# Four edits in a two-block fp32 transformer kernel: one attention stage for three branches, middle taps on ScalarE, key weights loaded once for two heads, modulation sums in the up part

## The chip, the cores and the metric

The kernel runs on one core of a Trainium2 chip, as one launch. The metric is the device time of the launch in microseconds (us). TensorE (PE) multiplies, VectorE (DVE) and ScalarE (ACT) compute elementwise, GpSimd (POOL) computes elementwise and issues some DMAs, SyncE (SP) issues the other DMAs. Each engine runs its own queue in order, and the engines meet at semaphores.

## The reference, cut to what matters

All tensors are fp32, with 256 context tokens, 256 latent tokens and a width of 1024. A first block has two decoder layers; each ends in a feed-forward net with a depthwise 3x3 convolution:

```python
def conv_ffn(h, w_up, conv_w, conv_b, w_down, grid):
    gate, up = jnp.split(h @ w_up, 2, axis=-1)
    gate = dwconv_grid(gate, conv_w, conv_b, grid)
    return (jax.nn.gelu(gate, approximate=True) * up) @ w_down
```

Layer 0 does it for 512 tokens, layer 1 for the 256 latent tokens. A second block has one layer of sparse attention with a SwiGLU net, and one layer whose attention has three branches over the same queries, 16 heads of 64 with 4 key heads:

```python
pc = masked_softmax(sc, cmp_end[None, :] <= t[:, None])   # 15 compressed keys
oc = jnp.einsum('bgrqn,bngd->bgrqd', pc.astype(vc.dtype), vc)
...
o = gb[..., 0:1] * oc.astype(F32) + gb[..., 1:2] * os_.astype(F32) + gb[..., 2:3] * ow.astype(F32)
```

At this length the selected branch and the window branch both see all earlier tokens. A mixture of experts follows. Every layer also needs its modulation vectors, `silu(c) @ w_ada[layer] + b_ada[layer]`, with a weight of 1024 x 6144.

## The kernel before, in words

The program is a chain of stages (`engines_block`). In a stage each engine has its own list of work; between stages all engines meet.

**Feed-forward, `ffn_stage` (L1677).** The up part runs 11 rounds. A round loads four weight tiles of 512 KB (two for the gate chunks in banks 0 and 1, two for the up chunks in banks 2 and 3) and PE fills banks 0 and 1, then 2 and 3. DVE copies the nine taps and the bias of a chunk out of `vec` (L1731, L1732), writes the middle tap and the bias (`tensor_scalar`, L1737), adds the eight other taps one after the other (L1747; with context tokens two more, L1739 and L1740), and frees the bank. ScalarE applies gelu (L1771), and DVE multiplies with bank 2 or 3 (L1756) and frees that. For layer 0 (`split`, 512 tokens) each weight tile is also cut into a high and a low part, by DVE (L246) and POOL (L298). PE may start on a bank only when it has been freed, and in the next round it wants bank 1 a quarter of a half-round after bank 0. The down part is `gemm_stage` (L953) with 4 rounds of four tiles.

**Modulation sums, `ModSums` (L526).** 12 groups of 512 columns; a group has 4 tiles of 512 KB that POOL loads into a ring (L559), and 8 `scalar_tensor_tensor` of 128x512 on DVE (L573), each waiting for the one before. For layer 1 of the first block all 12 groups run beside the down part (`in_background`). In `swiglu_stage` they run beside its up part. `mod_stage` (L714) then turns the sums.

**Small projections, `small_stage` (L2479).** For keys ("pair") the weight is laid out with the columns of a head twice, `[P, DC, n, 2, HD]`, so that one matmul group of 8 steps writes the head into both halves of the partitions; it takes 16 DMAs of 128 KB with runs of 64 numbers, ahead of which PE doesn't start, and one group for each head. Five key tensors of 4 heads and one of 1 head are made so: one of 4 and the one of 1 in the sparse layer, `k_cmp` and `v_cmp` in one stage, `k_slc` and `k_win` in the next.

**Attention, `attention_stage` (L2626).** 16 items, each a query block `b` and a pair of heads: `b`=0 has 128 keys, `b`=1 has 256, the compressed branch has 16 for both. PE scores (L2655), DVE scales, masks and takes the maximum (L2732, L2734), ScalarE takes the exponential (L2705), DVE divides and gates (L2719 to L2724), PE transposes (L2666), ScalarE copies (L2690), PE multiplies with the values (L2676), and ScalarE copies the output (L2697) or DVE adds it (L2740). DVE's order within step n is: norm of item n-1, mask of item n, output of item n-3. The branch layer calls the stage three times.

## Time and profile before

| | us |
|---|---|
| median of 3 runs | 4150.27 (4146.25 to 4158.99) |
| the profiled execution, its own time | 4148.6 |
| its span | 4146.7 |
| PE busy | 3445.2 (83%) |
| DVE busy | 2622.0 (63%) |
| ACT busy | 1443.2 (35%) |
| POOL busy | 1145.1 (28%) |
| mean granted TensorE clock | 0.898 of full |

A busy share is a mean over some hundred stages with different limits. What a stage is worth is read from that stage's own rows. Clock 1.00 is TensorE at 2.4 GHz, 0.50 is 1.2 GHz.

### The profile page before, as it was taken

How to read it: one execution, taken by the hardware profiler on the slowest of the kernel's cores; microseconds unless marked ns; L12 is line 12 of the kernel's file. 1: busy time of each engine (PE TensorE's matmuls, PEld its weight loads, DVE VectorE, ACT ScalarE, POOL GpSimd, SP SyncE). 2: the span in 40 equal slices, each digit the busy share in tenths (PEclk: the TensorE clock that was granted, in tenths of full speed). 3: DMA queues.
4: the chain of work that ended last, by engine and by line, in shares of the span. 5: the costliest groups of instructions: out<-in, count | busy, mean ns of one | idle time of the engine just before them, and what ended most of it. 6: DMA issues, size and time to landing. Idle time of an engine off the chain costs nothing. (4 is left out here: it accounts for less than half of the span.)

```text
span 4146.7 us, 71734 instructions
## 1 busy us (share of the span) xinstructions
PE 3445.2 (83%) x26140; PEld 2695.3 (65%) x26140; DVE 2622.0 (63%) x4214; ACT 1443.2 (35%) x2628; POOL 1145.1 (28%) x1074
## 2 busy tenths in 40 slices
PE   5897867999687888598576887777769999999997
PEld 2644446864464787487464776675547888888886
DVE  2437668889556445566545440235449999999997
ACT  1124321000205664100102100013237777777775
POOL 0000004432001220101200110000027778787785
PEclk8998978999799999799786998966879999999998
DMA  7310013247120000446531773320139999999995
GB/s 296 94 51 1 1 41 96 92 144 244 42 82 21 5 5 4 147 143 228 206 78 35 236 263 110 88 74 1 41 124 334 354 335 343 345 337 348 335 342 215
DMA packets 335179, 651.12 MB, mean 157 GB/s; under 512 B 68413, under 2 KB 193449, under 8 KB 334825
## 3 DMA queue, kind: packets, MB, share of 16 engines
q1 hardware_dynamic: 311193, 561.84, 39.6%
q0 software_dynamic: 23040, 83.90, 5.9%
q8 instruction: 160, 2.62, 0.3%
q10 hardware_dynamic: 720, 2.23, 0.1%
q14 instruction: 66, 0.54, 0.0%
HBM read 646.85 MB, written 1.05 MB: 156 GB/s over the span
## 5 line engine op out<-in xcount | busy, mean ns | idle before, releaser
L3279 DVE TENSOR_TENSOR weights_lo<-raw_ring,weights_hi 128x704 fp32r<-128x704 f32 (+1 forms) x376 | 451.4, 1242 | 58.5 <-ACT weights_hi L3240 57.7
L3161 POOL TENSOR_TENSOR weights_lo<-raw_ring,weights_hi 128x192 fp32r<-128x192 f32 (+1 forms) x376 | 403.8, 1088 | 120.9 <-ACT weights_hi L3240 95.5
L3240 ACT ACTIVATE weights_hi<-raw_ring 128x896 fp32r<-128x896 f32 (+1 forms) x376 | 364.1, 986 | 140.1 <-PE bank_pair L3216 129.9
L3216 PE MATMUL bank_pair<-weights_hi,expert_x_hi 128*128 128x512 f32 (+1 forms) x1024 | 308.6, 382 | 29.7 <-POOL weights_lo L3161 21.9
L323 PE MATMUL bank_pair<-H,ring_up 128*128 128x256 f32 x1408 | 310.8, 383 | 22.6 <-DMA ring_up<-in_ffn_w_gate 10.3
L323 PEld LDWEIGHTS bank_pair<-H,ring_up 128*128 128x128 f32 x1408 | 269.2, 192 | 63.8 <-DMA ring_up<-in_ffn_w_gate 10.5
L3279 DVE TENSOR_TENSOR weights_lo<-H,weights_hi 128x704 fp32r<-128x704 f32 (+1 forms) x240 | 292.5, 1261 | 16.4 <-ACT weights_hi L3240 16.4
L3216 PE MATMUL bank_pair<-weights_lo,expert_x_hi 128*128 128x512 f32 (+1 forms) x1024 | 294.5, 368 | 0.0
L3216 PE MATMUL bank_pair<-weights_hi,expert_x_lo 128*128 128x512 f32 (+1 forms) x1024 | 293.8, 368 | 0.0
L323 PE MATMUL bank_pair<-x_hi,ring_hi_in 128*128 128x512 f32 (+1 forms) x576 | 209.6, 364 | 94.6 <-DVE ring_lo_in L298 81.9
L3161 POOL TENSOR_TENSOR weights_lo<-H,weights_hi 128x192 fp32r<-128x192 f32 (+1 forms) x240 | 258.7, 1090 | 67.5 <-ACT weights_hi L3240 56.5
L3240 ACT ACTIVATE weights_hi<-H 128x896 fp32r<-128x896 f32 (+1 forms) x240 | 236.2, 993 | 71.7 <-PE bank_pair L3216 71.7
L323 PE MATMUL bank_pair<-ffn_h,ring_down 128*128 128x512 f32 (+1 forms) x704 | 235.6, 497 | 21.3 <-DMA ring_down<-in_ffn_w_down 17.1
L895 POOL TENSOR_TENSOR norm_work<-X 128x512 f32<-128x512 f32 x7 | 8.2, 1170 | 886.3 <-SPq L196 886.3
L3216 PEld LDWEIGHTS bank_pair<-weights_hi,expert_x_hi 128*128 128x128 f32 x1024 | 175.8, 189 | 79.8 <-DVE weights_lo L3279 28.5
L323 PEld LDWEIGHTS bank_pair<-ffn_h,ring_down 128*128 128x128 f32 x704 | 136.3, 195 | 120.2 <-issue 89.0
L323 PE MATMUL bank_pair<-x_lo,ring_hi_in 128*128 128x512 f32 (+1 forms) x576 | 205.6, 357 | 0.0
L323 PE MATMUL bank_pair<-x_hi,ring_lo_in 128*128 128x512 f32 (+1 forms) x576 | 205.5, 357 | 0.0
L3216 PEld LDWEIGHTS bank_pair<-weights_lo,expert_x_hi 128*128 128x128 f32 x1024 | 186.3, 188 | 24.5
L3216 PEld LDWEIGHTS bank_pair<-weights_hi,expert_x_lo 128*128 128x128 f32 x1024 | 186.7, 188 | 23.8
L323 PEld LDWEIGHTS bank_pair<-x_hi,ring_hi_in 128*128 128x128 f32 x576 | 113.6, 197 | 117.2 <-DVE ring_lo_in L298 85.0
L559 POOL DMA_DIRECT2D mod_ring_ada<-in_w_ada x96 | 69.4, 723 | 376.3 <-DVE mod_sums_ada L573 188.3
(632 smaller groups left out, 7409.0 us busy)
## 6 DMA issues: line engine op xcount, KB each, us to landing
raw_ring<-in_moe_w_gate SPq DMA_DIRECT2D x72, 896.0 KB, 6.7
raw_ring<-in_moe_w_up SPq DMA_DIRECT2D x64, 896.0 KB, 6.5
ring_up<-in_ffn_w_up SPq DMA_DIRECT2D x110, 512.0 KB, 3.5
mod_ring_ada<-in_w_ada POOLq DMA_DIRECT2D x96, 512.0 KB, 6.7
raw_ring<-in_moe_w_down SPq DMA_DIRECT2D x48, 1024.0 KB, 7.3
H<-in_moe_w_gate SPq DMA_DIRECT2D x40, 896.0 KB, 6.9
H<-in_moe_w_up SPq DMA_DIRECT2D x40, 896.0 KB, 6.1
H<-in_moe_w_down SPq DMA_DIRECT2D x32, 1024.0 KB, 7.6
```

The costliest lines, as they stand in the source:

```text
L323: ins = self.core.nc.tensor.matmul(self.banks[o][:, 0:moving.shape[1]], lhs, moving, start=(s == self.first[o] and k == 0 and i == 0), sto ...
L559: eng.dma_start(self.ring[:, s], self.w[:, k:k + self.PART, ds(g * self.WIDE, self.WIDE)]).then_inc(self.landed[s].sem, 16)
L895: nc.gpsimd.tensor_tensor(work[0][:, q], jobs[0].x(q), jobs[0].x(q), ALU.mult).then_inc(pool_squared.sem, 1)
L3161: nc.gpsimd.tensor_tensor(lo[:, u % CUTS, at].bitcast(F32R), raw_part(u)[:, at], hi[:, u % CUTS, at], ALU.subtract).then_inc(pool_parted.s ...
L3216: ins = nc.tensor.matmul(banks[half][:, 0:b - a], x, w[:, a:b], start=start and i == 0, stop=stop and i == 2)
L3240: nc.scalar.activation(hi[:, u % CUTS, 0:n].bitcast(F32R), raw_part(u), ACT.Copy).then_inc(cut.sem, 1)
L3279: nc.vector.tensor_tensor(lo[:, u % CUTS, 0:n].bitcast(F32R), raw_part(u)[:, 0:n], hi[:, u % CUTS, 0:n], ALU.subtract).then_inc(dve_parted ...
```

## The change

1. `ffn_stage`, both layers: the taps of both chunks are copied first; ScalarE writes the middle tap and the bias (Identity with a scale and a bias operand) and signals DVE, which adds the other taps. Gelu follows as before.
2. `ffn_stage`, layer 1 only: 11 of the 12 groups of modulation sums move from the down part to the up part, one group a round, in two halves of four, each ahead of one multiplication; POOL issues their loads there. One group stays beside the down part.
3. `small_stage`: key weights are loaded once, with one DMA of 1 MB; one matmul group makes two heads, and ScalarE copies each head into both halves, four copies a group.
4. `attention_stage`: the three branches are items of one stage (48 items), their outputs add up in PSUM; DVE masks item n before it norms item n-1; PE transposes item n-2 and multiplies item n-3; score tiles are threefold. The value matmuls have 64 columns a head, into one half of the output each. The sparse layer has 16 items and gets the same order.
5. In the branch for overfull experts a norm is added.

```diff
-                    c.ended(nc.vector.tensor_copy(taps[:, o, 9:10], st.vec[:, ds(b0 + n, 1)]))
-                    bank = g.wait_bank(dve, o, it)
-                    if not first:
-                        dve.wait_ge(gelu_ready.sem, gelu_ready.at(it * 2 + o - 1))
+                    nc.vector.tensor_copy(taps[:, o, 9:10], st.vec[:, ds(b0 + n, 1)]).then_inc(taps_ready.sem, 1)
+                for o in (0, 1):
+                    bank = g.banks[o]
+                    dve.wait_ge(middle_ready.sem, middle_ready.at(it * 2 + o + 1))
                     y = conv[:, o]
-                    c.ended(nc.vector.tensor_scalar(y, bank[:, 0:T], taps[:, o, 4:5], taps[:, o, 9:10], ALU.mult, ALU.add))
...
                 ahead(1)
                 for o in (0, 1):
+                    if sums:
+                        sums.add_group(dve, it, range(4 * o, 4 * o + 4))
                     bank = g.wait_bank(dve, 2 + o, it)
...
+                for o in (0, 1):
+                    act.wait_ge(taps_ready.sem, taps_ready.at(it * 2 + o + 1))
                     if not first:
                         act.wait_ge(g.free[2 + o].sem, g.free[2 + o].at(it))
+                    bank = g.wait_bank(act, o, it)
+                    nc.scalar.activation(conv[:, o], bank[:, 0:T], ACT.Identity, scale=taps[:, o, 4:5], bias=taps[:, o, 9:10]).then_inc(middle_ready.sem, 1)
+                for o in (0, 1):
+                    act.wait_ge(g.free[o].sem, g.free[o].at(it + 1))
                     nc.scalar.activation(gelu[:, o], conv[:, o], ACT.Gelu_apprx_tanh).then_inc(gelu_ready.sem, 1)
...
-    sums = beside()
+    if sums:
+        sums.part(n_it, sums.total)
+    else:
+        sums = beside()
...
+        def both_halves(bank, dst, g, heads):
+            for j in range(heads):
+                for half in (0, 1):
+                    ins = nc.scalar.activation(dst[half * HD:(half + 1) * HD, g + j], bank[j * HD:(j + 1) * HD], ACT.Copy)
...
-                t = core.sb(f"w_pair{i}", [P, DC, n, 2, HD], ctx=ctx)
+                t = core.sb(f"w_pair{i}", [P, DC, n * HD], ctx=ctx)
+                for g in range(0, n, 2):
...
-                if kind == "pair":
-                    for k in range(DC):
-                        for a in (0, 1):
-                            loaded[i].count(sp.dma_start(ws[i][:, k, :, a], ...), 16)
+                width = n if kind == "tokens" else n * HD
+                loaded[i].count(sp.dma_start(ws[i][:], v[:, :, col:col + width]), 16)
...
+            for n in range(N + 3):
                 if n < N:
+                    score(n)
+                if 0 <= n - 2 < N:
+                    turn(n - 2)
+                if 0 <= n - 3:
+                    add(n - 3)
...
+                        ins = nc.tensor.matmul(OUT[g % 2][h * HD:(h + 1) * HD, 0:P], br.v[0:w, j, hp * 2 // group, HD:2 * HD], pt[0:w, n % 2, h * 2 + j],
+                                               start=i == 0 and j == 0, stop=i == B - 1 and j == last)
...
+            for n in range(N + 4):
+                if 0 <= n - 2 < N:
+                    copy_turned(n - 2)
+                if n < N:
+                    expo(n)
+                if 0 <= n - 4 and (n - 4) % B == B - 1:
+                    copy_out((n - 4) // B)
...
+            for n in range(N + 1):
+                if n < N:
+                    mask(n)
+                if n:
+                    norm(n - 1)
...
+        attention_stage(core, st, q, [Branch(kc, vc, cmp_neg, CMP_STRIDE, branch(0), cmp_seen), Branch(k_slc, v_slc, seen, gate=branch(1)),
+                                      Branch(k_win, v_win, seen, gate=branch(2))], out)
```

## Rows read from the trace of the kernel before

**Rows 1.** Windows of both up parts: busy of each engine, clock, DMA.
```profile
core 0: us, PE busy (x) PEld busy (x) DVE busy (x) ACT busy (x) POOL busy (x), PEclk, DMA share, GB/s
660.00:890.00 230.00, 228.85 (x1010) 189.18 (x1008) 202.59 (x344) 13.85 (x22) 102.63 (x40) 1.00 0.27 85
...
1760.00:1920.00 160.00, 154.27 (x699) 132.14 (x698) 99.61 (x261) 8.86 (x22) 0.00 (x0) 1.00 0.43 134
```

**Rows 2.** Timeline, layer 1's up part: start, length, instruction, idle before.
```profile
1766.68 0.54 DVE L1737 TENSOR_SCALAR conv<-bank_pair,taps 128x256 f32<-128x256 f32 x1 [12.53 <-PE bank_pair L323]
1767.25 3.70 DVE L1747 SCALAR_TENSOR_TENSOR conv<-bank_pair,taps,conv 128x189 f32<-128x189 f32 x8
...
1775.46 14.08 PE L323 MATMUL bank_pair<-H,ring_up 128*128 128x256 f32 x64 [0.27 <-DVE conv L1747]
1789.92 10.41 PE L323 MATMUL bank_pair<-H,ring_up 128*128 128x256 f32 x47 [0.38 <-DVE conv L1747]
...
1920.41 0.42 DVE L1756 TENSOR_TENSOR ffn_h<-conv,bank_pair 128x256 f32<-128x256 f32 x1 [0.23 <-ACT conv L1771]
```

**Rows 3.** Eight sum steps in the timeline; Identity of 256 columns in the groups.
```profile
2002.93 6.27 DVE L573 SCALAR_TENSOR_TENSOR mod_sums_ada<-mod_ring_ada,act,mod_sums_ada 128x512 f32 x8 [1.32 <-DMA mod_ring_ada<-in_w_ada]
...
L836 ACT ACTIVATE H<-norm_work,mod,coef 128x256 f32<-128x256 f32 x72 | 36.1, 586 | 24.6 <-DVE norm_work L885 24.6
```

**Rows 4.** Timeline: PE's start in layer 1's up part and in SwiGLU's.
```profile
1757.46 17.73 PE L323 MATMUL bank_pair<-H,ring_up 128*128 128x256 f32 x72 [8.65 <-DMA ring_up<-in_ffn_w_up]
...
2314.03 31.23 PE L323 MATMUL bank_pair<-H,ring_up 128*128 128x256 f32 x135 [10.31 <-DMA ring_up<-in_ffn_w_gate]
```

**Rows 5.** Timeline: layer 1's down part, and the first matmuls behind it.
```profile
1925.36 15.79 PE L323 MATMUL bank_pair<-ffn_h,ring_down 128*128 128x256 f32 x64 [7.42 <-DMA ring_down<-in_ffn_w_down]
...
1971.74 19.26 PE L323 MATMUL bank_pair<-ffn_h,ring_down 128*128 128x256 f32 x88 [0.60 <-ACT Y L1777]
...
2032.61 3.64 PE L743 MATMUL bank_pair<-mod_sums_ada,const 128*32 128x512 f32 x16 [21.76 <-PEq L196]
```

**Rows 6.** Timeline, layer 0's up part: a copy of taps while POOL computes.
```profile
872.00 2.36 DVE L1731 COPY taps<-vec 128x9 f32<-128x9 f32 x1
```

**Rows 7.** Small projections: timeline of SP and PE, and a DMA's landing.
```profile
2111.71 8.61 SPq L2512 DMA_DIRECT2D w_pair<-in_a_w_in  x16
...
2123.11 15.79 PE L2531 MATMUL bank_pair<-H,w_pair 128*128 128x256 f32 x64 [12.91 <-DMA w_pair<-in_a_w_in]
...
2589.99 29.98 PE L2531 MATMUL bank_pair<-H,w_pair 128*128 128x256 f32 x128 [15.94 <-DMA w_pair<-in_w_kv]
...
w_tokens<-in_w_kv SPq DMA_DIRECT2D x1, 1024.0 KB, 6.5
```

**Rows 8.** Windows of attention, columns as in Rows 1.
```profile
2211.46:2225.03 13.57, 11.15 (x50) 8.77 (x50) 6.73 (x20) 6.38 (x29) 0.00 (x0) 0.50 0.00 0
2245.63:2255.85 10.22, 5.91 (x44) 4.68 (x44) 6.43 (x13) 5.21 (x18) 0.00 (x0) 1.00 0.00 0
2817.28:2848.98 31.70, 27.37 (x120) 18.28 (x120) 11.98 (x72) 13.32 (x72) 0.00 (x0) 0.50 0.00 1
2855.73:2861.29 5.56, 3.32 (x16) 2.47 (x16) 3.02 (x11) 2.29 (x10) 0.00 (x0) 0.50 0.00 0
...
2206.22:2259.90 53.68, 39.23 (x208) 29.55 (x208) 28.20 (x64) 26.13 (x97) 0.00 (x0) 0.69 0.00 1
2807.69:2963.95 156.26, 110.32 (x576) 80.72 (x576) 84.03 (x288) 64.85 (x257) 0.00 (x0) 0.68 0.00 1
2231.97:2235.84 3.87, 3.13 (x12) 2.19 (x13) 2.15 (x5) 1.74 (x6) 0.00 (x0) 0.50 0.00 0
```

**Rows 9.** The window in which the clock rises in the sparse layer's attention.
```profile
2238.00:2243.00 5.00, 3.79 (x24) 2.54 (x22) 2.98 (x6) 2.52 (x10) 0.00 (x0) 0.87 0.00 0
```

**Rows 10.** Timeline: PE's value and score matmuls of one step at clock 0.50.
```profile
2217.95 1.06 PE L2676 MATMUL bank_pair<-pt,v 128*128 128x128 f32 x4
2218.94 0.80 PE L2655 MATMUL bank_pair<-kd,q 64*128 64x128 f32 x4
```

More of the change, by code:

```diff
@@ L2524, in _ @@
         def _(pe):
-            for m, (i, operands, width, _) in enumerate(outs):
+            for m, (i, operands, rows, width, _) in enumerate(outs):
                 pe.wait_ge(loaded[i].sem, loaded[i].at(loaded[i].n))
@@ L2530, in _ @@
                     lhs, rhs = operands(k)
-                    ins = nc.tensor.matmul(core.bank(m % 4)[:, 0:width], lhs, rhs, start=k == 0, stop=k == DC - 1)
+                    ins = nc.tensor.matmul(core.bank(m % 4)[0:rows, 0:width], lhs, rhs, start=k == 0, stop=k == DC - 1)
                 ready.count(ins)
@@ new lines, in score @@
+            def score(n):
+                b, hp, i = items[n]
+                br = branches[i]
+                if n >= 2:
+                    pe.wait_ge(masked.sem, masked.at(n - 1))
+                for h in (0, 1):
+                    half = slice(h * HD, (h + 1) * HD)
+                    ins = nc.tensor.matmul(SC[n % 2][:, h, 0:br.keys(b)], q[half, hp, b * P:(b + 1) * P],
+                                           br.k[half, hp * 2 // group, 0:br.keys(b)], start=True, stop=True)
+                ins.then_inc(scored.sem, 1)
@@ new lines, in turn @@
+            def turn(n):
+                b, hp, i = items[n]
+                pe.wait_ge(normed.sem, normed.at(n + 1))
+                if n >= 2:
+                    pe.wait_ge(pt_ready.sem, pt_ready.at(n - 1))
+                for h in (0, 1):
+                    for j, (at, w) in enumerate(branches[i].blocks(b)):
+                        ins = nc.tensor.transpose(TR[n % 2][0:w, (h * 2 + j) * P:(h * 2 + j + 1) * P], s[:, n % 3, h, at:at + w], st.C("ident"))
+                ins.then_inc(turned.sem, 1)
@@ new lines, in add @@
+            def add(n):
+                b, hp, i = items[n]
+                br, g = branches[i], n // B
+                pe.wait_ge(pt_ready.sem, pt_ready.at(n + 1))
+                if i == 0 and g >= 2:
+                    pe.wait_ge(out_taken.sem, out_taken.at(g - 1))
+                last = len(br.blocks(b)) - 1
+                for j, (_, w) in enumerate(br.blocks(b)):
+                    for h in (0, 1):
+                        ins = nc.tensor.matmul(OUT[g % 2][h * HD:(h + 1) * HD, 0:P], br.v[0:w, j, hp * 2 // group, HD:2 * HD], pt[0:w, n % 2, h * 2 + j],
+                                               start=i == 0 and j == 0, stop=i == B - 1 and j == last)
+                ins.then_inc(summed.sem, 1)
@@ new lines, in copy_out, with expo @@
+            def copy_out(g):
+                b, hp = pairs[g]
+                act.wait_ge(summed.sem, summed.at((g + 1) * B))
+                nc.scalar.activation(out[:, hp, b * P:(b + 1) * P], OUT[g % 2][:, 0:P], ACT.Copy).then_inc(out_taken.sem, 1)
+            def expo(n):
+                b, hp, i = items[n]
+                act.wait_ge(masked.sem, masked.at(n + 1))
+                if n >= 2:
+                    act.wait_ge(normed.sem, normed.at(n - 1))
+                for h in (0, 1):
+                    x = s[:, n % 3, h, 0:branches[i].keys(b)]
+                    ins = nc.scalar.activation(x, x, ACT.Exp, bias=low[:, n % 2, h:h + 1], accum_out=total[:, n % 2, h:h + 1])
+                ins.then_inc(exped.sem, 1)
@@ new lines, in norm @@
+            def norm(n):
+                b, hp, i = items[n]
+                br = branches[i]
+                K = br.keys(b)
+                x, r = s[:, n % 3, :, 0:K], total[:, n % 2]
+                dve.wait_ge(exped.sem, exped.at(n + 1))
+                c.ended(nc.vector.reciprocal(r, r))
+                if br.gate is not None:
+                    c.ended(nc.vector.tensor_tensor(r, r, br.gate[:, b, 2 * hp:2 * hp + 2], ALU.mult))
+                if br.some is not None:
+                    c.ended(nc.vector.tensor_tensor(x, x, br.some[:, b, 0:K].unsqueeze(1).to_broadcast([P, 2, K]), ALU.mult))
+                nc.vector.tensor_tensor(x, x, r.unsqueeze(2).to_broadcast([P, 2, K]), ALU.mult).then_inc(normed.sem, 1)
```

192 lines of the change are left out of this document (74 added, 118 removed).

## The prediction, on record before the result was known

> **What bounds the kernel now.** I read the page first, then the windows of each stage that the diff touches, then the timeline inside it. The page's shares decide nothing here: every edited stage has its own limit.
>
> Layer 0's up part is PE's: 228.85 us busy of 230.00, clock full; DVE has 202.59 [rows 1]. Layer 1's up part is nearly PE's: a round starts every 14.46 us (1775.46 to 1789.92), of which 14.08 is matmul and 0.38 a wait for DVE's last tap [rows 2]. Between bank-ready and that last tap DVE does two middle taps of 0.54 and two chains of 3.70. DVE is busy 99.61 of 160 us there and the DMA engines 0.43 of the time [rows 1], so there is room for something. In layer 1's down part PE has done its four rounds 21.76 us before the next matmul, which comes at 2032.61 [rows 5]: PE idles there while the sums finish. The small projections wait 11.4 us for sixteen DMAs (2111.71 to 2123.11) [rows 7]. Attention is a serial round trip: in five items of 128 keys DVE is busy 6.73 of 13.57 us, ACT 6.38, PE 11.15 at half clock; in three items of 256 keys at full clock nobody is busy more than 6.43 of 10.22 [rows 8].
>
> **Attention.** The new order lets DVE mask item n while ScalarE is at item n-1, so the round trip goes and the busiest engine sets the pace. DVE's busy time an item, plus 0.1 for gaps between dependent instructions (an estimate): 128 keys 6.73/5+0.1=1.45; gated 3.02/2+0.1=1.61; 256 keys 6.43/3+0.1=2.24, gated some 2.4; compressed 11.98/12+0.1=1.1 [rows 8]. ScalarE has 6.38/5=1.28, 5.21/3=1.74 and 13.32/12=1.11, less than DVE over a triple. PE is the question: at half clock it has 11.15/5=2.23 an item of 128 keys and 27.37/12=2.28 a compressed one, more than DVE; at full clock 5.91/3=1.97 even for 256 keys, less [rows 8]. Its value matmuls now fill half the array's columns each: of the 2.23 the value step is 0.99 (2217.95 to 2218.94) [rows 10]. It costs between half of that, if the two halves run side by side as the two heads' scores do (four score records in 0.80 [rows 10]), and all of it; I take 1.9 an item. The clock stood at 0.50 through the whole compressed stretch, but rose some 30 us into the sparse stage (0.87 in 2238 to 2243 [rows 9]), with PE still pausing there. PE will now pause less; I take 20 us at half clock in the sparse stage and 25 in the branch stage.
>
> The Trainium skill, TensorEngine Tiling, Theoretical Speedup, says that a stationary side of at most 64 columns gives up to twice the speed. By it the value step would be 0.5 and the item 1.7, 2 to 3 us less over both stages; the rows here show no such matmul.
>
> Start and end of a stage: 53.68 less eight items of 2.71 and eight of 3.41 leaves 4.7 [rows 8], kept. Sparse: 8x1.45+8x2.24+4.7=34.2, and for the slow clock 8x0.45+1.3=4.9 more: 39.1, against 53.68, so -14.6. Branch: a triple is 1.1+2x1.61=4.3 or 1.1+2x2.4=5.9; 8x(4.3+5.9)+4.7=86.3, and four triples at half clock (2.28+2x1.9=6.1) cost 1.8 each: 93.5, against 156.26, so -62.8. Together -77.4. Ends: full clock from the start -89; half clock throughout (2.23 and, from the 3.87 window with its 3.13 of PE, 3.6 an item [rows 8]) only -24.
>
> **Small projections.** 64 more records cost 29.98-15.79=14.2, so a group of 16 costs 3.5 [rows 7]. Five tensors of four heads go from four groups to two: ten groups fewer, -35 (the weights of the second head pair ride along; ScalarE's four copies a group, 0.4 each, hide behind 3.5 of matmul, except the last group of one stage, +0.8). Three stages wait for the first tensor; a single DMA of 1024 KB landed in 6.5 us amid others [rows 7]. I take 5.9 from first issue to first matmul instead of 11.4: -5.5 each, -16.5. Two loads in the same queue may share it (7.6, twice 1 MB), or it may land in 5; so 45 to 53 saved, -50.2 taken.
>
> **Layer 1's up part.** DVE's round becomes: copies of taps for the first chunk 0.22; handover to ScalarE, an Identity with two operands of 0.59 (586 ns [rows 3]) and back, 0.7, during which the other copies hide; two chains of 3.62; eight sum steps 6.27 [rows 3]; two multiplications of 0.38. That is 15.2. The sum steps sit ahead of the multiplications, so gelu hides behind them. PE's 14.08 is now less than DVE's round: banks 0 and 1 are freed at 4.5 and 8.2 us of it, banks 2 and 3 at 11.7 and 15.2, each before PE wants it, so DVE alone sets the pace. Behind DVE waits POOL: each tile summed lets it issue the next load, and DVE's small copies may wait for that; unseen, between 0 and 2.9 (four copies, 0.72 an issue) a round. I take 15.3. Up part, from first bank ready to last multiplication: before 1920.83-1766.68=154.2, after 10x15.3+15.2=168.2: +14.0. Its start: with sum tiles loaded beside, SwiGLU's first matmul came 10.31 us after the norm's last, here it was 8.65 [rows 4]: +1.7. The memset of the sums hides in that wait. The DMA engines then go from 0.43 busy to what SwiGLU has, where PE never waited.
>
> The Trainium skill, SBUF — State Buffer, "SBUF: two separate sides", speaks against this edit: a DVE copy in its two-port mode keeps POOL from writing descriptors, so DMAs issued there start late. By it each load would start up to 0.2 us late, and with a ring of a whole group the sum stays the same.
>
> **Layer 1's down part.** Before, from the last multiplication to the first matmul behind: 2032.61-1920.83=111.8. After: PE starts as before after 4.5, a first round 21.3 (19.26 and 2.0 for the low clock after the pause; the two megabytes left beside it land in time at the rate that weights had), three rounds of 19.86, then ScalarE's copies and the meeting, 1.3: 86.7. So -25.1 [rows 5]. The two parts together: -9.4. Bounds -3 (a DMA wait in the first round, longer rounds) and -14.
>
> **Layer 0's up part.** DVE loses 2x0.81 a round and waits for ScalarE 0.85 instead; PE covers it. If PE's cover is gone it costs what DVE has beyond 21.8 a round. One thing may take it: a small copy waited 2.36 us for POOL's work [rows 6], and now two stand one behind the other, up to 2.4 more a round, against a slack of some 2.5. I take -0.6, for the shorter tail, and +15 as the other end. The norm in the overfull branch costs nothing: that branch was not entered (1024 records of each gate matmul, one pass over eight experts).
>
> **Sum.** -77.4-50.2-9.4-0.6=-137.6; 4148.6-137.6=**4011 us**, and as the profiled time is 1.7 below the median of the runs, the same against that.
>
> **Rivals.**
> - *PE stays at half clock in attention.* For it: the compressed stretch never rose, and a third of the new items are such. Against: two dense items follow each. Costs 53 more: 4064. Chance 0.07; a middle case, low through the whole first half of the branch stage (4 more triples, 7 us) is inside the forecast.
> - *Full clock at once and halved value steps.* -12: 3999. Chance 0.12.
> - *DVE's small copies queue behind POOL.* Layer 1 +13 or so, layer 0 up to +15: 4039. For it: the 2.36 us copy [rows 6]. Against: at layer 0 the copies already wait and PE doesn't. Chance 0.12.
> - *The clock falls wherever PE pauses in each period.* This ends on the other side. PE would pause 1.2 us in every round of layer 1's up part; at half clock a round is 28.2 us, 12.9 more, +142, and attention stays slow, +53: 4206. It decides once about ten of the eleven rounds are slow and attention too. Against: PE was busy only 5.91 of 10.22 us in attention with the clock at 1.00 [rows 8]. Chance 0.03.
> - *The moved sums buy nothing,* as the round grows by all that the down part gives back (2.3 us a round more): 4020, inside the range. Counted in the forecast's spread.
>
> The Trainium skill, ScalarE: Activation LUTs, Table sets, holds that identity is in every table set, so ScalarE wouldn't reload between Identity and gelu; no row here shows the two in turn. With a reload (1.28 us each at the start of stages) twice a round, layer 1 would be at some 18 a round and the whole at about 4040.
>
> **Numbers.** Forecast 0.64, the four priced rivals 0.34, anything else 0.02. The range leaves out the slow end and holds the third rival: 3988 to 4044. Under 0.3% (12 us) this kernel's measurement can't tell a change. Faster 0.96, same 0.01, slower 0.03.
>
> **What would show it.** Attention: one stage of 94 us and one of 39, DVE idle only in short gaps, PE at 1.00 in the second half. Small projections: one DMA for each key tensor, first matmul 6 us after the first issue. Layer 1: rounds of 15.3 with PE waiting for DVE, and no tail of sums after the down part's last matmul. Layer 0: rounds still 21.8. The prediction is wrong if PE stays at 0.50 in attention, if ScalarE loads tables in the up part, or if DVE's copies stretch a round.

## The result and the profile after

The changed kernel took **4062.53 us** (median of 4 runs, 4058.09 to 4067.58), the kernel before 4154.63 beside it: ratio 0.9771, 95% interval 0.975 to 0.9791. It is faster, but by 92 us and not 138, and the time lies outside the forecast's range (3988 to 4044). The profiled executions have spans of 4064.4 and 4146.7, so 82.3 us between them have a place.

The first reading is a budget of stages. All engines meet between two stages (L196), and the time from one meeting to the next, read at PE's wait there, is a stage's length, also where nothing was edited:

```
                                    before    after   change   forecast
start to layer 0's up part           635.9    641.5    +5.7       0
layer 0's up part                    255.2    254.5    -0.7      -0.6
up to layer 1's up part              862.7    870.1    +7.3       0
layer 1's up part                    167.2    177.5   +10.2     +15.7
layer 1's down part                  111.5     85.8   -25.7     -25.1
the three stages behind it            79.1     74.1    -5.1       0
small projections (three stages)     138.2    90.9    -47.4     -50.2
sparse attention                      53.9     37.6   -16.4     -14.6
branch attention                     156.6    109.5   -47.1     -62.8
expert stage                        1044.0   1084.6   +40.6       0
all other stages                     642.4    638.5    -3.7       0
```

(The last digits are rounded apart.) Windows of the changed kernel over layer 1's up part and down part, the sparse attention, the branch attention and the expert stage; columns as in [rows 1]:

```profile
1766.10:1943.60 177.50, 156.57 (x704) 134.49 (x704) 154.55 (x331) 21.66 (x45) 31.79 (x44) 0.96 0.77 260
1943.60:2029.30 85.70, 78.64 (x352) 67.78 (x352) 6.01 (x8) 2.63 (x8) 2.88 (x4) 0.95 0.49 159
2188.00:2225.60 37.60, 33.12 (x208) 18.91 (x208) 27.50 (x64) 26.89 (x97) 0.00 (x0) 0.70 0.00 1
2733.10:2842.60 109.50, 97.72 (x576) 55.40 (x576) 75.97 (x256) 65.30 (x257) 0.00 (x0) 0.63 0.00 1
2953.40:4038.00 1084.60, 1024.33 (x4768) 858.96 (x4768) 942.43 (x904) 780.27 (x881) 810.44 (x744) 0.98 0.91 326
```

Against [rows 1] DVE is now busy 154.55 of 177.50 us in the up part. PE is busy 156.57, so the shares don't decide; the timelines do: in a round DVE has no idle time but 0.65 us, and PE waits for DVE's last tap. DVE sets the pace there, as forecast. In attention, against [rows 8], PE is the busiest engine, at a granted clock of 0.63. The largest surprise is the last window: in the expert stage no line was edited. The same window of the kernel before:

```profile
3076.20:4120.30 1044.10, 1011.20 (x4768) 845.92 (x4768) 963.07 (x904) 780.45 (x881) 818.12 (x744) 1.00 0.94 338
```

The same instructions (x4768, x904, x881, x744), 40 us more. A timeline of GpSimd at the start of the second expert, before and then after:

```profile
3208.34 1.41 POOL L3161 TENSOR_TENSOR weights_lo<-const,weights_hi 128x224 fp32r<-128x224 f32 x1
3209.71 3.14 POOL L3156 TENSOR_TENSOR expert_x_lo<-seated,expert_x_hi 128x1024 fp32r<-128x1024 f32 x1
```

```profile
3084.36 1.38 POOL L3233 TENSOR_TENSOR weights_lo<-const,weights_hi 128x224 fp32r<-128x224 f32 x1
3090.66 2.35 POOL L3228 TENSOR_TENSOR expert_x_lo<-seated,expert_x_hi 128x1024 fp32r<-128x1024 f32 x1 [4.92 <-issue]
```

Now GpSimd stands 4.92 us and waits for nothing that the profile shows ("issue"). At the third expert the pause is 4.63, and PE's timeline behind it reads:

```profile
3229.17 1.11 PE L3288 MATMUL bank_pair<-weights_hi,expert_x_hi 128*128 128x512 f32 x2 [5.53 <-POOL weights_lo L3233]
3230.08 0.95 PE L3288 MATMUL bank_pair<-weights_hi,expert_x_lo 128*128 128x512 f32 x2
...
3234.56 0.65 PE L3288 MATMUL bank_pair<-weights_hi,expert_x_lo 128*128 128x512 f32 x2
3235.05 0.57 PE L3288 MATMUL bank_pair<-weights_lo,expert_x_hi 128*128 128x512 f32 x2
```

PE waits 5.53 us for GpSimd's part of the weights, and then runs its matmuls at 0.95 in place of 0.57 us for another 5 us. The granted clock is low there; the window behind the pause, columns as in [rows 1]:

```profile
3229.00:3235.00 6.00, 5.83 (x16) 5.12 (x17) 2.28 (x3) 1.89 (x2) 3.57 (x5) 0.52 1.00 375
```

An expert takes 134.8 us (3090.66 to 3225.50) where it took 128.8, and the pause comes seven times: 42 us, against 40.6 by which the stage grew. Two other views give the trail. The list of waits of the changed kernel in that stage (who waits, for whom, us in total, times, longest) has the line below; and in the list of DMA queues on the page (packets, MB, share) one queue stands out, shown for the kernel before and then for the changed one:

```profile
POOL expert_x_lo L3228 <- issue: 32.6, 7, 5.3
```

```profile
q14 instruction: 66, 0.54, 0.0%
```

```profile
q14 instruction: 136, 1.11, 0.1%
```

One queue that carries instructions has 70 packets more. By their times, 83 lie in the expert stage, against 11 before, many of them around the start of each expert. So the theory to test: **GpSimd's loop over the experts no longer fits into what the engine holds of its program, and is loaded anew for each expert.** In the built program that loop has 282 instructions instead of 228 (the traces record the same numbers in a round, from one branch to the next), both times from place 454 of GpSimd's program. The work is the same; the difference is 54 register additions. Each wait of the loop compares a semaphore with a threshold that is computed in a register, and the counters start where the stages before left them. Before, the thresholds of the counter `cut` coincided with thresholds of `used` 34 steps earlier, and the build reused the register; with other stages in front they don't coincide.

### The profile page after: what moved, and what is told of

It reads as the page before. It is cut to its first block and busy times, and to the rows that moved or that the text cites. A ratio compares the mean times of both kernels' runs of the same rounds, so it can differ in the third digit from the quotient of the medians.

```text
span 4064.4 us, 70956 instructions
## 1 busy us (share of the span) xinstructions
PE 3414.1 (84%) x25980; PEld 2642.5 (65%) x25980; DVE 2568.1 (63%) x4138; ACT 1478.0 (36%) x2693; POOL 1137.4 (28%) x1074
## 5 line engine op out<-in xcount | busy, mean ns | idle before, releaser
L3351 DVE TENSOR_TENSOR weights_lo<-raw_ring,weights_hi 128x704 fp32r<-128x704 f32 (+1 forms) x376 | 438.7, 1205 | 101.2 <-ACT weights_hi L3312 100.5
L3351 DVE TENSOR_TENSOR weights_lo<-H,weights_hi 128x704 fp32r<-128x704 f32 (+1 forms) x240 | 283.1, 1216 | 26.5 <-ACT weights_hi L3312 26.2
L1760 DVE SCALAR_TENSOR_TENSOR conv<-bank_pair,taps,conv 128x189 f32<-128x189 f32 (+2 forms) x352 | 151.0, 432 | 24.9 <-ACT conv L1791 13.2
```

Of the source, the lines that this page charges most:

```text
L1760: ins = nc.vector.scalar_tensor_tensor(yg[:, rows[0], rows[1]], xg[:, from_[0], from_[1]], taps[:, o, w:w + 1], yg[:, rows[0], rows[1]], A ...
L3351: nc.vector.tensor_tensor(lo[:, u % CUTS, 0:n].bitcast(F32R), raw_part(u)[:, 0:n], hi[:, u % CUTS, 0:n], ALU.subtract).then_inc(dve_parted ...
```

## Experiments

### Is it GpSimd's loop?

**moe_cut_apart**: one number in the kernel before.

```diff
+        ahead = 1000
+        cut.base += ahead
...
+            act.sem_inc(cut.sem, ahead)
```

> The kernel before, with one number changed in the expert stage: the counter that ScalarE's cuts signal starts 1000 higher. In the built program this takes GpSimd's expert loop from 228 to 282 instructions, the length it has in the changed kernel, because a threshold computed for one wait is no longer reused for another one; nothing else in the loop changes. Theory 1 (the changed kernel loses some 40 us in the untouched expert stage since GpSimd's longer loop is loaded anew for each expert): the expert stage goes from 1042 to about 1083 us, GpSimd stands 4 to 5 us ahead of the first subtraction of experts 2 to 8, its instruction queue shows some 80 packets there, and the whole is at about 4190. Theory 2 (the loss comes from slower weight transfers or a different clock): 4150, the expert stage stays at 1042. Theory 3 (the norm added in the branch for overfull experts): 4150 too.

**moe_thresholds_shared**: the reverse, in the changed kernel.

```diff
+        apart = cut.base - (used.base + UNITS - CUTS - 34)
+        cut.base, used.base = cut.base + max(0, -apart), used.base + max(0, apart)
...
-            pe.sem_inc(used.sem, UNITS)
+            pe.sem_inc(used.sem, UNITS + max(0, apart))
...
+            if apart < 0:
+                act.sem_inc(cut.sem, -apart)
```

> The changed kernel, with the starting values of two counters of the expert stage moved so that thresholds are reused as in the kernel before: GpSimd's expert loop is back at 228 instructions, the arithmetic is the same. Theory 1 (loop loaded anew for each expert): expert stage back from 1083 to 1042 us, the whole at about 4022. Theories 2 (slower transfers) and 3 (the added norm): no change, 4063.

**moe_loop_moved**:

```diff
+        if len(branches) > 1:
+            idle = core.sb("idle", [P, 64], ctx=ctx)
+            @block.gpsimd
+            def _(pool):
+                for i in range(64):
+                    nc.gpsimd.memset(idle[:, i:i + 1], 0.0)
```

> The changed kernel with 64 memsets of one column on GpSimd while the branch attention runs, where GpSimd has nothing to do. GpSimd's expert loop keeps its 282 instructions, but starts 64 instructions later in the program. If it is the length by itself (more register instructions in each step), nothing comes back: 4063. If it is the place of the loop together with its length, that is, whether it fits into what the engine holds of its program at one time, the pause of 4.7 us ahead of each expert goes and the whole is at about 4022. Theories 2 (slower transfers) and 3 (the added norm): 4063. The Trainium skill, Runtime: NRT & Kernel Launch, Instruction fetch mechanics, says that the engine holds two blocks of 256 instructions and that a branch out of them waits for a load; by it a loop of 282 would fit again once it is moved by 64.

**no_rare_norm**:

```diff
         with core.rarely(route.most[0:1, 0:1], SEATS):
-            norm_in(core, st, 2, 24)
```

> The changed kernel without the norm that was added in the branch for overfull experts, which is not entered with this input. Theory 3 (that norm changes where the expert loop stands): 4022. Theories 1 (length and place of GpSimd's loop, which stands ahead of it) and 2 (slower transfers): 4063, the expert stage at 1083.

Measured, with the length and place of GpSimd's expert loop in the built program and the expert stage of the profile:

```
                        loop  starts  expert stage   median us   ratio to before (95%)
before                   228     454        1044.0
changed                  282     454        1084.6     4062.53   0.9771 (0.975 to 0.9791)
moe_cut_apart            282     454        1084.9     4190.01   1.0094 (1.0067 to 1.0122)
moe_thresholds_shared    228     454        1047.7     4019.07   0.9671 (0.9651 to 0.9692)
moe_loop_moved           282     520        1042.8     4009.12   0.9653 (0.9629 to 0.9678)
no_rare_norm             282     454        1086.1     4053.14   0.9754 (0.9731 to 0.9778)
```

One number in the kernel before makes it 39 us slower; the same kind of number takes 37 us off the expert stage of the changed kernel (to 1047.7; the last 3.7 us didn't come back in that profile, and did in all others). The added norm is innocent, as it was forecast to cost nothing; without it the kernel took 4053.14 us, 44 more than moe_loop_moved on the same chip. And the loop of 282 is as fast as the short one when it merely stands 66 places later. So it is not the extra instructions themselves, it is where they lie. In moe_cut_apart VectorE's loop grew as well, from 221 to 224 instructions; moe_loop_moved keeps that and moves GpSimd's alone, so it is GpSimd's that counts. The list of waits of moe_cut_apart has the pause, in the kernel before's own code:

```profile
POOL expert_x_lo L3158 <- issue: 35.2, 7, 5.8
```

One part of the expectation failed. The instruction queue was to show some 80 packets in the expert stage, and showed 47, in the whole run 102. The versions of the changed kernel without a pause have 100 to 102 too, also those with a loop of 195 instructions, and the ones with the pause 136 or 137. So the pause adds 35 or 36 packets, to 66 or to 101, and the other half of the 70 comes with the changed kernel in some other way, which is open. The packets alone don't tell a pause; the "issue" waits do.

Two more runs look for the border. They change only the number of memsets, to 16 and to 32.

**loop_at_472**

> The changed kernel with 16 instead of 64 one-column memsets ahead; with two branches around them GpSimd's expert loop of 282 instructions starts at place 472 of its program instead of 454. What is known: start 454 is slow, start 448 is not, start 520 is not. If the loop must lie within two neighbouring blocks of 256 instructions, a block ends between 730 and 735 (ends of the loops at 448 and 454), so others end at 218 to 223 and 474 to 479: a loop that starts at 472 and ends at 754 reaches into a third block, and the expert stage is at 1084. If the 6 instructions between 448 and 454 mattered in another way (any small shift repairs it), it is at 1043.

**loop_at_488**

> The same with 32 memsets: the loop starts at 488, behind the border at 474 to 479, and so lies in two blocks again, though it ends 34 instructions beyond the loop that is slow. By the two blocks the expert stage is at 1043. If what counts is how far into the program the loop reaches, up to some distance between 488 and 520, it is at 1084.

The starting point of that reasoning is the run sums_stay_down (below), whose loop of 282 starts at 448. All in order of place:

```
                  starts    ends   expert stage   median us
sums_stay_down       448     730         1042.5     4018.34
changed              454     736         1084.6     4062.53
loop_at_472          472     754         1095.6     4051.02
loop_at_488          488     770         1044.5     4013.98
moe_loop_moved       520     802         1042.8     4009.12
```

Fast, slow, slow, fast, fast, as two neighbouring blocks of 256 demand with block ends at some place between 730 and 735 and 256 earlier: a distance limit or a general sensitivity to shifts would not let it be slow at 472 and fast at 488. In loop_at_472 (two timed runs, as loop_at_488) the pauses are there again, 31.2 us in 7 times, and in loop_at_488 there are none. But loop_at_472 has a second pause in each round, 15.6 us in 7 times, and its expert stage is 11 us longer than the changed kernel's. GpSimd's timeline at the start of its fourth expert:

```profile
3338.69 2.35 POOL L3235 TENSOR_TENSOR expert_x_lo<-seated,expert_x_hi 128x1024 fp32r<-128x1024 f32 x1 [4.29 <-issue]
3343.40 2.24 POOL L3240 TENSOR_TENSOR weights_lo<-raw_ring,weights_hi 128x192 fp32r<-128x192 f32 x4 [2.36 <-issue]
```

The trace records the register operations between the two as well: the sixth instruction of the round starts at 3338.75 and the seventh, which is place 478, at 3343.38. In the changed kernel, whose loop starts 18 places earlier, the seventh follows the sixth in 0.1 us. So the border can be seen, at 478, inside the 474 to 479 that was worked out beforehand, and it lies 252 to 257 places ahead of the one between 730 and 735. The Trainium skill, Runtime: NRT & Kernel Launch, Instruction fetch mechanics, describes just this: two blocks of 256 instructions, and a taken branch out of them waits for a load. These runs agree with that rule. The price here, some 4.7 us on GpSimd and 6 us on the expert's period, is the runs' own.

### The parts by themselves

**attention_alone**: the kernel before with edit 4 alone.

> The kernel before with the fourth edit alone: the three branches in one stage, masks ahead of scales, half-column value matmuls, in the sparse layer too. If the parts add up, the sparse attention stage goes from 53.5 to 38 us and the three branch stages from 157 to 108, together 64, and nothing else moves: 4151-64=4087. In the built program GpSimd's expert loop has 196 instructions here, so by theory 1 (the loop's length and place) the expert stage stays at 1042 to 1046; if a change in front of the expert stage costs those 40 us in some other way, it is at 1084 and the whole at 4127.

It took 4082.29 us, ratio 0.9849 (0.9824 to 0.9874), 63 less than the kernel before beside it (4145.23): sparse 38.7, branch 109.8, expert stage 1043.4. The part adds up.

**sums_stay_down**: the changed kernel with

```diff
-        sums = None if split else beside()
+        sums = None
```

> The changed kernel without the second edit: all twelve groups of modulation sums stay beside layer 1's down part, the middle taps stay on ScalarE. If the moved sums are worth what the stages show (up part +10.2, down part -25.5), the up part is at some 167 us instead of 177.8 and the down part at 111.4 instead of 85.9, and the whole at 4063+15=4078. If DVE's rounds were held up by the handover to ScalarE and not by the sums, the up part stays near 178 and the whole is at 4088. GpSimd's expert loop has 282 instructions here too and starts 6 instructions earlier than in the changed kernel: the expert stage stays at 1084 by theory 1, unless those 6 just let it fit.

4018.34 us, ratio 0.969 (0.9662 to 0.9719). Without edit 2 the changed kernel is faster: by 44.8 us between the profiled spans, by 34 going by the ratios, since the kernel before took 9 us less beside this run. Both totals that were foreseen, 4078 and 4088, were far off, because the expert stage was fast (1042.5): the six places did let the loop fit. The up part is at 160.0, less than either theory had, the down part at 111.6. PE's timeline of that up part has no wait left in it:

```profile
1789.68 50.67 PE L323 MATMUL bank_pair<-H,ring_up 128*128 128x256 f32 x234
```

So ScalarE's middle tap alone is worth 7.2 us there (167.2 to 160.0). The moved sums cost 17.5 in the up part (177.5) and give 25.8 in the down part and 5.0 in the stage behind it (11.6 to 6.6): 13.3 gained. And they put six more instructions into GpSimd's program, which push the expert loop over the border: 42 us lost. A gain of 13 turns into a loss of 29 at a place 900 us further on. The rest of the 44.8 lies in stages whose code is the same in both: 10.0 from layer 0's up part to layer 1's (870.1 against 860.1), 3.0 each in the branch attention (106.5) and the first small projections (28.7).

### Why the branch attention took 109 us

In the changed kernel PE is the bound while the clock is low. Windows of the narrow half (pairs of 128 keys) and the wide half (256 keys), and one narrow triple in PE's timeline:

```profile
2733.10:2783.60 50.50, 48.94 (x256) 26.19 (x256) 35.28 (x138) 31.71 (x137) 0.00 (x0) 0.50 0.00 1
2783.60:2842.60 59.00, 48.78 (x324) 29.21 (x322) 40.69 (x119) 33.59 (x120) 0.00 (x0) 0.73 0.00 1
```

```profile
2765.59 0.61 PE L2705 MATMUL bank_pair<-kc,q 64*128 64x16 f32 x4
2766.21 0.69 PE L2716 MATMUL bank_pair<-const,scores 128*128 128x128 f32 x2
2766.83 0.69 PE L2728 MATMUL bank_pair<-pt,vc 16*64 16x128 f32 x4
2767.45 0.80 PE L2705 MATMUL bank_pair<-k_slc,q 64*128 64x128 f32 x4
...
2771.30 0.61 PE L2705 MATMUL bank_pair<-kc,q 64*128 64x16 f32 x4
```

PE is busy 48.94 of 50.50 us, and its clock stays at 0.50 all the same.

**late_blocks_first** and **blocks_in_turn** change the order of the items, in the version with the moved loop:

```diff
-    pairs = [(b, hp) for b in (0, 1) for hp in range(HEADS // 2)]
+    pairs = [(b, hp) for b in (1, 0) for hp in range(HEADS // 2)]                # late_blocks_first
+    pairs = [(b, hp) for hp in range(HEADS // 2) for b in (0, 1)]                # blocks_in_turn
```

> The changed kernel with GpSimd's loop moved by 64 instructions (the version measured at 4009), and with the eight items pairs of 256 keys ahead of the eight of 128 in both attention stages. Theory A: the clock rises with the kind of work, and the narrow items of 128 keys hold it at 0.50; then it rises within the first 20 us of the branch stage and falls back in its second half, and the stage takes about what it takes now, 108 us, within 5. Theory B: the clock needs some 50 us of attention before it rises, whatever the items; then the wide items run at 0.50 throughout, 8.6 us a triple, the narrow ones at 1.00 with DVE's pace of 4.3 to 4.6, and the stage takes 8*8.6+8*4.5+5=110 us. The two differ in the clock by half: A gives high then low, B low then high.

> The same version, with the pairs of 128 and 256 keys in turn. If the wide items raise the clock and it then stays up through one narrow triple, the whole stage but its first part runs at 1.00: a pair of triples at DVE's pace 4.4+6.5=10.9, eight of them and 5 for the ends 92 us, some 16 less than now, and 3 less in the sparse layer: about 3990. If the narrow items pull the clock down each time, the stage takes 8*(5.7+8.6)+5=119 us: 4020. In between it stays at 4009.

Windows of late_blocks_first, the second ten us, and then two stretches in its narrow half:

```profile
2720.00:2730.00 10.00, 8.90 (x69) 5.17 (x68) 7.93 (x24) 6.50 (x23) 0.00 (x0) 0.81 0.00 1
...
2780.00:2790.00 10.00, 9.97 (x54) 5.36 (x52) 6.88 (x27) 6.04 (x29) 0.00 (x0) 0.50 0.00 0
2790.00:2800.00 10.00, 9.97 (x56) 5.37 (x54) 7.46 (x32) 6.25 (x27) 0.00 (x0) 0.50 0.00 1
```

Theory A holds here: the clock is up with the wide items and down with the narrow ones, though PE is busiest in these. The branch stage is at 104.2 and the sparse one at 34.0 (107.7 and 38.6 in the version with the moved loop); 3999.51 us, ratio 0.9644 (0.9617 to 0.9671). In turn, the clock doesn't stay up: windows of 20 us through the stage show 0.55 to 0.70. The stage takes 112.6 us, nearer to the 119 than to the 92, and the whole 4010.38.

What is it about the narrow items? The change itself halved the columns of the value matmuls.

**values_full_width** gives them back:

```diff
-                        ins = nc.tensor.matmul(OUT[g % 2][h * HD:(h + 1) * HD, 0:P], br.v[0:w, j, hp * 2 // group, HD:2 * HD], pt[0:w, n % 2, h * 2 + j],
-                                               start=i == 0 and j == 0, stop=i == B - 1 and j == last)
+                        ins = nc.tensor.matmul(OUT[g % 2][:, 0:P], br.v[0:w, j, hp * 2 // group, (1 - h) * HD:(1 - h) * HD + P], pt[0:w, n % 2, h * 2 + j],
+                                               start=i == 0 and j == 0 and h == 0, stop=i == B - 1 and j == last and h == 1)
```

> The version at 4009 (moved loop), with the value matmuls of both attention stages as the kernel before has them: 128 columns with a zero half, both heads into one accumulation, instead of 64 columns into one half each. If TensorE sets the pace in the narrow items (it was busy 9.97 of 10 us at clock 0.50), each of the 24 narrow items of the branch stage costs what the matmuls take more: value step 0.99 instead of 0.70, 0.3 us an item at half clock, 7 us over the first half, and some 2 to 5 in the second half: the stage at 117 instead of 108. If the round trip or DVE sets the pace, it stays at 108.

More work for PE, and the stage got shorter: 99.5 us (two timed runs). Neither answer that was foreseen came. Three further runs follow it up, all with the short loop of GpSimd (`34` of moe_thresholds_shared replaced by `1`, which makes it 195 instructions).

**short_loop_half_values**

> The changed kernel with the short expert loop of GpSimd (195 instructions) and nothing else; the partner for the next two on the same chip. Every theory so far: expert stage 1043 to 1047, branch attention 106 to 110 with the clock at 0.50 through its narrow half, the whole at 4009 to 4022.

**short_loop_full_values**

> The same with value matmuls of 128 columns, half of them zero, as the kernel before had them. Theory C: the 64-column value matmuls are what holds the clock at 0.50, since they leave half of the array without work; with 128 columns it rises in the narrow half too (0.80 and more from 20 us into the stage on), and the branch stage is at 99 to 101 again. Theory D: the 99.5 of the one profile was a lucky place of the clock, and the stage is at 106 to 110.

**full_values_late_first**

> The same with 128 columns and with the 256-key items first. By theory C the clock is up after the first 15 us and stays up, and the branch stage takes 8 wide triples at 6.5 and 8 narrow at 4.5 and some 8 for the start and the ends, 96 us, the sparse stage 34: the whole some 15 below its half-column partner in this call. If the order brings nothing once the clock holds, it is 99 and 37, and the whole 9 below.

Windows of the branch stage, its second fifth, the kernel with half columns and then the one with full columns:

```profile
2749.60:2771.80 22.20, 22.16 (x119) 11.99 (x118) 15.43 (x62) 13.96 (x63) 0.00 (x0) 0.50 0.00 1
```

```profile
2744.50:2764.40 19.90, 17.37 (x125) 13.16 (x124) 15.79 (x66) 14.82 (x67) 0.00 (x0) 0.91 0.00 1
```

```
                          values  order         sparse   branch   median us   ratio to before (95%)
short_loop_half_values      64    narrow first    37.6    111.0     4018.15   0.9667 (0.9649 to 0.9686)
short_loop_full_values     128    narrow first    36.7     99.4     4013.26   0.9665 (0.964 to 0.9689)
values_full_width          128    narrow first    36.7     99.5     4008.45   0.9652 (0.9614 to 0.9691)
late_first_short_loop       64    wide first      34.4    108.5     4007.25   0.9657 (0.9631 to 0.9683)
full_values_late_first     128    wide first      36.7    106.4     4016.69   0.9656 (0.9636 to 0.9677)
```

In the change's own order the runs came out as theory C said: with 128 columns the clock is at 0.91 in the second fifth and the stage takes 99.4 and 99.5 us, against 105.3 to 111.1 in all eight profiles of that order with 64 columns inside the changed kernel's other edits. That the gain is the clock's, and not that of a cheaper step, can be read triple by triple, from PE's first compressed score matmul of a triple to that of the next (us; the first and the last triple of each kind left out):

```
                      at 0.50       at 1.00
narrow,  64 columns   5.72          4.2 to 4.5   (changed; late_blocks_first, late_first_short_loop)
narrow, 128 columns   6.62          4.3 to 4.8   (full_values_late_first; the runs with 128 columns)
wide,    64 columns                 5.8 to 6.5   (changed; late_blocks_first, late_first_short_loop)
wide,   128 columns                 6.1 to 6.7   (the runs with 128 columns)
```

At the same clock the full columns are never clearly quicker, and at 0.50 they cost 0.9 us a triple.

With the wide items first, 128 columns bring nothing that can be told: 106.4 us lies between the 104.2 and 108.5 of the two profiles with 64, and the sparse stage is some 2.5 longer (36.7 against 34.0 and 34.4). full_values_late_first was expected at 96. A narrow triple of it, with 128 columns and PE never idle, stands at 0.50 as well:

```profile
2812.80:2819.40 6.60, 6.60 (x31) 5.05 (x30) 3.97 (x17) 3.54 (x18) 0.00 (x0) 0.50 0.01 1
```

So with the wider value matmuls the clock was higher in one order of the items and not clearly in the other. Why is open, and with it what keeps the clock down.

**late_first_short_loop** is the version that was meant to beat both kernels.

> The changed kernel with the 256-key items first in both attention stages and with the starting values of two counters of the expert stage set so that a threshold is reused in the next step: GpSimd's expert loop has 195 instructions in place of 282, and fits whatever stands ahead of it. Expert stage 1043 (1084 in the changed kernel), attention stages 34 and 104 (38 and 109): 4063-41-9=4013 by those, and as the version with moved loop and late blocks first came out at 3999.5, 4000 to 4013. If the shorter loop also lets GpSimd part the weights sooner and that were on the path, it would be under 3990.

It did: 4007.25 us (4000.65 to 4015.64), ratio 0.9657, inside the expected 4000 to 4013, though its branch stage came out at 108.5 and not 104. The five versions of the last table all lie within 11 us and their intervals overlap: gains of 5 to 10 us in one stage can't be told apart in the whole, and stand on the stages' lengths alone.

## Why the prediction was right or wrong, by its own steps

**The step that failed** is the one that put no price on untouched stages. The change's part 5, "The norm in the overfull branch costs nothing", was right (no_rare_norm). But the prediction costed instructions only where they run, and 54 register additions in GpSimd's expert loop had no term. They cost 40.6 us in the expert stage, at a place (454) that is the same as before; the six loads that edit 2 adds to GpSimd's program keep the loop there, as it fits without them (448). The rest of the prediction missed by 14.8 together (4066.35 us of the profiled execution less 4011 is 55.4). moe_loop_moved, which computes what the changed kernel does and only moves that loop, took 4009.12 us against the forecast of 4011. That agreement is partly luck: the branch attention was mis-sized by 15.7 to one side, the edits of layer 1 by 6 and the stage behind them by 5 to the other.

**Attention, sparse**: -14.6 forecast, -16.4 measured. The mechanism (pipelined order, the busiest engine sets the pace) and the size hold.

**Attention, branch**: the mechanism held and a size was off, the time at half clock: "I take 20 us at half clock in the sparse stage and 25 in the branch stage". It was 50.5 us at 0.50 and 59.0 at 0.73 on average. At half clock a narrow triple takes 5.72 us (2765.59 to 2771.30; forecast 6.1) for eight of them and not four, and a wide triple some 7.4 (59.0 over eight) where 5.9 was taken. 109.5 against 93.5. The argument "PE will now pause less", so the clock rises sooner, is refuted: PE paused hardly at all and the clock stayed low. The rival of half clock throughout had the clock of the narrow half right and that of the wide half wrong. The middle case, low through the whole first half, was priced at 7 us; the other 9 are 1.5 a triple in the wide half, less 0.4 on each narrow one.

**Half-column value matmuls**: the step takes 0.62 us at half clock (2766.83 to 2767.45; the dense one of 128 rows 0.63), and 0.66 was assumed. The size was right; that the clock differs with it was not foreseen, and in the change's order the stage lost more than the step saved: 107.7 us with half columns and 99.5 with full ones on one base, 111.0 and 99.4 on the other.

**Small projections**: -50.2 forecast, -47.4 measured. (The prediction's terms, -35, +0.8 and -16.5, add up to -50.7.) In the timeline of SP and PE of the changed kernel the first key load is issued at 2103.48 and PE starts at 2109.31, 5.8 us later (5.9 forecast):

```profile
2103.48 0.37 SPq L2546 DMA_DIRECT2D w_pair<-in_a_w_in  x1
...
2109.31 2.93 PE L2562 MATMUL bank_pair<-H,w_pair 128*128 128x256 f32 x6 [7.34 <-DMA w_pair<-in_a_w_in]
```

The two stages for keys and values gave 18.5 and 19.0, near the 19.5 that four groups and a start make; the sparse one 9.9 here and 12.6 to 12.9 in seven of the thirteen other runs that have this edit.

**Layer 1's up part**: the round takes 14.96 us, 15.3 forecast. Two starts of rounds in DVE's timeline of the changed kernel:

```profile
1794.75 7.32 DVE L1760 SCALAR_TENSOR_TENSOR conv<-bank_pair,taps,conv 128x189 f32<-128x189 f32 x16 [0.65 <-ACT conv L1791]
...
1809.71 2.35 DVE L1760 SCALAR_TENSOR_TENSOR conv<-bank_pair,taps,conv 128x189 f32<-128x189 f32 x5 [0.65 <-ACT conv L1791]
```

The handover to ScalarE takes 0.65 us (0.7 forecast), and nothing is lost to queued copies. The later start of 1.7 didn't come either: PE waited 8.74 us for the first tile, 8.65 before [rows 4]. So +10.2 against +15.7. **The down part**: -25.7 against -25.1; from the last multiplication (which ends at 1943.37) to the first matmul behind it (2029.45), 86.1 against 86.7. The stage behind it, `mod_stage`, had no term and took 6.6 us where it took 11.6; its granted clock was 1.00 and had been 0.50.

**Layer 0's up part**: -0.7 against -0.6. The rival's mechanism was there all the same. Before, one of the two nine-tap copies of a round took 2.36 us [rows 6]; now both do, in all eleven rounds:

```profile
726.74 2.36 DVE L1745 COPY taps<-vec 128x9 f32 x1
729.02 0.14 DVE L1746 COPY taps<-vec 128x1 f32 x1
729.08 2.36 DVE L1745 COPY taps<-vec 128x9 f32 x1
```

DVE loses 2.2 us more a round, and PE's work covers it: rounds are still 21.8 us apart (726.74 to 748.53). The slack of some 2.5 us that the prediction counted was just enough.

**Rivals**: in layer 1 DVE's copies didn't queue behind GpSimd (0.11 to 0.17 us each); in layer 0 twice as many took 2.36 us, without a price. The clock did not fall in layer 1's up part (0.96 over the stage). "The moved sums buy nothing" missed in both directions: they buy 13 us and cost 42 elsewhere. ScalarE loads its table once in the up part (1.28 us, at 1780.11) and not in each round. The Trainium skill, ScalarE: Activation LUTs, Table sets, has identity in every table set, so that it had to be so; the trace agrees.

**What the budget leaves**: +13.0 in untouched stages ahead of layer 1. The sum of these stages (to the up part of layer 0, and from its end to layer 1) is 1498.6 before, 1502.5 in moe_cut_apart and 1511.6 in the changed kernel, but anything from 1490.7 to 1511.6 in the other kernels that share the changed kernel's code up to there. Much of it goes with the clock, as the window of one such stage shows, before and then after (0.94 and 0.82):

```profile
1253.80:1315.30 61.50, 46.51 (x128) 16.57 (x128) 54.50 (x72) 31.47 (x47) 0.00 (x0) 0.94 0.15 35
```

```profile
1258.70:1322.40 63.70, 51.70 (x128) 18.09 (x128) 54.78 (x72) 31.68 (x47) 0.00 (x0) 0.82 0.15 33
```

But 5.1 of the 13.0 lie in the longest of these stages (342.5 before, 347.6 after), with the clock at 0.97 both times; it took from 334.9 to 350.1 in the other profiles, whatever the clock. Why is open.

## What to carry to other kernels

Where a stage with a long loop runs slower and no line of it was edited, look for "issue" waits at the start of each round, and count the loop in the built program: its length can change through the starting values of recycled counters, and its place through six instructions far ahead. More packets in an instruction queue are a hint and no proof. Keep the body of a long loop short: at 195 and 228 instructions it paused from no place that was run. Don't save PE columns for speed at low clock without looking at the clock: a busy share near 1 did not raise it here.

## What the runs showed of the hardware

- A loop of 282 instructions on GpSimd ran without pause from places 448, 488 and 520 and paused in each round from 454 (4.7 us) and 472 (4.5 us and, between places 477 and 478, 2.2 us).
- With PE busy 22.16 of 22.20 us on matmuls of 64 rows, 64 columns and transposes, the granted clock stayed at 0.50; with value matmuls of 128 columns, half of them zero, it was 0.91 in the same fifth of the stage with PE busy 17.37 of 19.90. With the items in the other order it stood at 0.50 with 128 columns too (PE busy 6.60 of 6.60). The Trainium skill, TensorEngine Tiling, Theoretical Speedup, promises up to twice the speed for such columns; the step itself went from 0.99 to 0.62 us at equal clock, and the stage as a whole, in the change's own order, got slower by 6 to 12 us across the profiles.
- Stages with the same code differ from execution to execution: the sum of 21 of them lay between 1490.7 and 1511.6 us. Most of them are longer where the granted clock is lower; the longest is not.
